# Decoder layer on one core: inputs laid out ahead of the launch, the squares of x summed from a feature-major x, the decay's clip on ScalarE

## The chip, the cores and the metric

The kernel runs on one core of a Trainium2 chip. A core has four compute engines that run their own instruction lists side by side: TensorE (PE, matrix products), VectorE (DVE), ScalarE (ACT) and GpSimd (POOL); SyncE (SP) and ACT issue transfers (DMA) from main memory into SBUF, the on-chip memory of 128 partitions. Products land in PSUM. The engines wait for one another by semaphores. The metric is the device time of one execution in microseconds (us).

## The reference

One layer of a decoder with three kinds of heads, on x of 256 tokens by 2048 features, all in float32:

```python
h = rms_norm(x, norm_w)                       # x * rsqrt(mean(x*x) + 1e-6) * w
proj = jnp.einsum('btd,de->bte', h, w_in)     # all heads' q, k, v and gates
qkv = jax.nn.silu(causal_depthwise_conv(gqkv, conv_w))
o_ret  = retention(rq, rk, rv)                # 4 heads
o_gdn  = gated_delta_rule(gq, gk, gv, g, beta)# 6 heads, chunks of 64
o_moba = moba_attention(mq, mk, mv)           # 6 heads
y = concat([rms_norm(o_ret) * silu(rg), rms_norm(o_gdn) * silu(gz), o_moba * silu(mz)])
return x + jnp.einsum('bte,ed->btd', y, w_out)
```

In the gated delta rule `decay = exp(g_cum[i] - g_cum[j])` for i >= j, and a unit lower-triangular system is solved per chunk. The norm's weights multiply features, its rsqrt multiplies tokens, so the kernel projects x * w first and scales the result by the rsqrt (`rb`) afterwards.

## The kernel before

**Precision.** Each weight tile (128 partitions x 1024) is split into a high part (`w_hi`, a rounded copy, on ACT: `high_part`, L489) and a low part (`w_lo` = raw - high, on DVE: `low_part`, L369); x is split in the same way (`hT[:, k, 0]` and `hT[:, k, 1]`). A product is high x both halves of x plus low x the high half of x.

**Streaming.** There are 160 weight tiles, 8 per group, 20 groups (16 for the heads, 4 for the output). PE runs 64 "units" per group, 8 per tile: a unit is a 512-column and a 256-column matmul in the first groups (L1532 and L1533, or L1528 and L1529 for a bank's last). The other products (gates, chunks, attention) are put between units. Every engine's order is written by hand in terms of PE's unit number: `advance(u)` issues on ACT, DVE and POOL whatever belongs before unit u. In DVE's list the low part of tile n stands at unit 8 (n - 3) + 4, in ACT's the high part at 8 (n - 3); SP loads a tile as soon as one of the 8 buffers of `w_raw` is free. Each engine works its list in sequence and stops at a wait.

**The first group** (units 0 to 63) is written apart, since x has to be prepared beside it. Token-major x is loaded into `big`, in five pieces between the tiles (`load_piece`). PE transposes it in blocks of 128 (`x_block`, L1581) into PSUM, one set of four ahead of every tile; ACT makes the high half from PSUM (`x_high`, L576), DVE the low half from PSUM and the high half (L1016); POOL adds the two back into `whole` (L864, 16 instructions of 256 columns), which the 32 narrow gate products read (`ab_products`, L1670). The sums of squares are taken from token-major x by ACT (L557, tokens 0 to 127) and DVE (L1002, tokens 128 to 255), four pieces each; DVE makes the mean (L1031), POOL the power -1/2 (L851), PE spreads it over partitions (L1659), DVE copies it to `rb` (L1033). Parameters arrive as rows (`prow`) and are turned by PE (L1629, L1675). At the end DVE adds the halves of the first products and scales them (L1040, L1042), and later ones are added and scaled on POOL (L888, L892).

**Later.** `decay_clip` (DVE, L1167) forms min(g_cum difference, 0) for four 128 x 128 blocks of a pair of heads, ACT takes the exponent (L642). `inverse_of_pairs` (DVE, L1202 and L1205) prepares the solve of a pair of heads; the solve starts at unit 290. POOL's 512-wide subtraction L868 is part of the heads' outputs at 195 us and later.

## Time and profile before

| | us |
|---|---|
| median of 3 executions (lowest, highest) | 511.75 (511.47, 512.03) |
| the profiled execution | 511.29 |
| its span, first to last instruction | 509.5 |
| PE busy | 504.4 (99%) |
| DVE busy | 342.9 (67%) |
| ACT busy | 275.5 (54%) |
| POOL busy | 162.3 (32%) |

The profiled execution lasts 1.8 us longer than its span, for what lies before the first and behind the last instruction. The granted clock of TensorE was 0.999 of full speed in the mean. A row of the timeline gives the start, the busy time of the instructions that it groups (x2, x8: so many alike in a row), engine, line, what it writes and reads with partitions x columns, and in brackets the idle time before it with what ended it. The busy spans of neighbours overlap a little: a successor may start before the row of the one ahead of it ends.

### The profile page before, as it was taken

To read this page: it belongs to the slowest core of one execution; us is meant where nothing else is said; L and a number is where in the kernel's file an instruction comes from. 1 tells how busy PE (TensorE), PEld (TensorE's weight loads), DVE (VectorE), ACT (ScalarE), POOL (GpSimd) and SP (SyncE) were. 2 spreads that over 40 slices of the span, in tenths; PEclk is the share of its full clock that TensorE was granted. 3 is DMA by queue.
4 is the path that set the end of the run, shared out by engine and by line. 5 is a ranking of instruction groups with operands and counts; after the bars stand their busy time and mean duration, and the time that the engine had idled before them with its cause. 6 is when DMAs were issued, how large, how long until landed. Compare 5 with 4: busy or idle time off the path is not lost.

```text
span 509.5 us, 8939 instructions
## 1 busy us (share of the span) xinstructions
PE 504.4 (99%) x3442; PEld 424.6 (83%) x3442; DVE 342.9 (67%) x529; ACT 275.5 (54%) x452; POOL 162.3 (32%) x220
## 2 busy tenths in 40 slices
PE   8999999999999999999999999999999999999997
PEld 7888888888888888888888888888888888888885
DVE  5989999989776876565467455755567566646451
ACT  5776565754357676564537354564556456343340
POOL 5763343416121312135054105506050614230000
PEclk9999999999999999999999999999999999999999
DMA  8997656665744465563975676777775557767711
GB/s 283 344 313 207 166 133 165 185 173 142 200 124 130 126 165 144 146 183 69 303 185 156 160 221 169 187 207 195 186 193 169 166 172 231 219 186 225 256 43 41
DMA packets 154989, 92.62 MB, mean 182 GB/s; under 512 B 15971, under 2 KB 143938, under 8 KB 154946
## 3 DMA queue, kind: packets, MB, share of 16 engines
q1 hardware_dynamic: 151456, 89.86, 63.3%
q10 hardware_dynamic: 3490, 2.18, 1.5%
q8 instruction: 27, 0.44, 0.3%
q14 instruction: 16, 0.13, 0.1%
HBM read 89.00 MB, written 2.10 MB: 179 GB/s over the span
## 4 chain that ended last, share of the span: by engine, by line
PE 99%; POOL 0%; DVE 0%; DVEq 0%; issue 0%; POOLq 0%
PE pj L1554 20%; PE pj L1557 20%; PE pj L1556 20%; PE pj L1532 14%; PE pj L1533 7%; PE pj L1610 3%; PE pj L1619 1%; PE mx L1714 1%; PE pj L1529 1%; PE mx L1581 1%; PE mx L1749 1%; PE mx L1767 1%; PE pj L1627 1%; PE mx L1825 1%; PE mx L1887 1%; PE pj L1528 1%
## 5 line engine op out<-in xcount | busy, mean ns | idle before, releaser
L369 DVE TENSOR_TENSOR w_lo<-w_raw,w_hi 128x1024 fp32r<-128x1024 f32 x160 | 200.0, 1258 | 78.0 <-ACT w_hi L489 77.3
L489 ACT ACTIVATE w_hi<-w_raw 128x1024 fp32r<-128x1024 f32 x158 | 166.1, 1057 | 120.5 <-PE pj L1557 103.7
L1554 PE MATMUL pj<-w_hi,hT 128*128 128x512 f32 x320 | 126.4, 395 | 0.0
L1556 PE MATMUL pj<-w_hi,hT 128*128 128x512 f32 x320 | 126.1, 394 | 0.0
L1557 PE MATMUL pj<-w_lo,hT 128*128 128x512 f32 x320 | 124.7, 390 | 0.0
L1532 PE MATMUL pj<-hT,w_hi 128*128 128x512 f32 x300 | 109.3, 404 | 0.0
L1533 PE MATMUL pj<-hT,w_lo 128*128 128x256 f32 x300 | 83.9, 280 | 0.0
L1557 PEld LDWEIGHTS pj<-w_lo,hT 128*128 128x128 f32 x320 | 60.1, 188 | 12.2
L1554 PEld LDWEIGHTS pj<-w_hi,hT 128*128 128x128 f32 x320 | 60.1, 188 | 12.1
L1556 PEld LDWEIGHTS pj<-w_hi,hT 128*128 128x128 f32 x320 | 60.2, 188 | 11.5
L1532 PEld LDWEIGHTS pj<-hT,w_hi 128*128 128x128 f32 x300 | 56.3, 188 | 14.1 <-DVE w_lo L369 1.6
L917 POOL COPY mT<-mT 32x128 f32<-32x128 f32 x80 | 40.4, 506 | 60.1 <-issue 45.7
L1533 PEld LDWEIGHTS pj<-hT,w_lo 128*128 128x128 f32 x300 | 56.6, 189 | 0.5
L851 POOL TENSOR_TENSOR sm<-sm,cst 128x4 f32<-128x4 f32 (+2 forms) x12 | 15.8, 1313 | 111.7 <-DVE sm L1392 39.3
L1554 PE MATMUL pj<-w_hi,yT 128*128 128x512 f32 x128 | 50.3, 393 | 0.0
L1557 PE MATMUL pj<-w_lo,yT 128*128 128x512 f32 x128 | 49.8, 389 | 0.0
L1556 PE MATMUL pj<-w_hi,yT 128*128 128x512 f32 x128 | 49.8, 389 | 0.0
L888 POOL TENSOR_TENSOR ev<-ev 128x256 f32<-128x256 f32 x22 | 23.8, 1083 | 76.0 <-ACT ev L504 76.0
L917 POOL COPY kq<-mT 32x128 f32<-32x128 f32 x56 | 32.0, 571 | 11.2 <-DVE mT L1355 8.0
L1060 DVE SCALAR_TENSOR_TENSOR big<-raw,pcol,big 128x256 f32<-128x256 f32 x54 | 33.0, 613 | 1.4
L1557 PEld LDWEIGHTS pj<-w_lo,yT 128*128 128x128 f32 x128 | 24.0, 188 | 5.1
L1556 PEld LDWEIGHTS pj<-w_hi,yT 128*128 128x128 f32 x128 | 24.0, 188 | 4.9
(238 smaller groups left out, 537.6 us busy)
## 6 DMA issues: line engine op xcount, KB each, us to landing
w_raw<-in_w_in_dram SPq DMA_DIRECT2D x256, 256.0 KB, 3.3
w_raw<-in_w_out_dram SPq DMA_DIRECT2D x64, 256.0 KB, 4.0
...
```

Source lines behind the costliest of these rows:

```text
L369: eng.tensor_tensor(w_lo[:, n % NSPLIT, :], w_raw[:, n % NRAW, :], w_hi[:, n % NSPLIT, :].bitcast(F32), ALU.subtract).then_inc(S("lo"), 1)
L489: act.activation(w_hi[:, n % NSPLIT, :], w_raw[:, n % NRAW, :], ACT.Copy).then_inc(S("hi_done"), 1)
L851: return pool.tensor_tensor(sm[:, dst:dst + n], sm[:, src:src + n], cst[:, K_POW:K_POW + n], ALU.pow)
L888: pool.tensor_tensor(ev[:, n % 2, 0:T], ev[:, n % 2, 0:T], ev[:, n % 2, T:2 * T], ALU.add).then_inc(S("halves"), 1)
L917: ins = pool.tensor_copy(dst[i:i + QUART, :, a:a + QUART], src[a:a + QUART, :, i:i + QUART])
L1060: ins = dve.scalar_tensor_tensor(dst, raw_of(j, h, i, slice(k, k + T)), tap, dst, ALU.mult, ALU.add)
L1532: pe.matmul(pj[s][:, :], high, hT[:, kc].rearrange("p a t -> p (a t)"), start=first, stop=False)
L1533: ins = pe.matmul(pj[s][:, 0:T], low, hT[:, kc, 0, :], start=False, stop=False)
L1554: ins = pe.matmul(bank[:, :], src[:, kc, 0, tok], hi[:, k, :], start=first, stop=False)
L1556: pe.matmul(bank[:, :], src[:, kc, 1, tok], hi[:, k, :], start=False, stop=False)
L1557: ins = pe.matmul(bank[:, :], src[:, kc, 0, tok], lo[:, k, :], start=False, stop=last)
L1610: pe.matmul(pj[s][:, cols], block_of(hi, 0, s, k), hT[:, TK * t + k].rearrange("p a t -> p (a t)")[:, cols], start=t == 0 and a == 0, stop ...
```

## The change

The host now lays the inputs out before the launch:

- x also goes in feature-major (`turned_x`, 128 x 4096), so that `load_piece` brings it straight into `whole`, in seven pieces; the first two are issued on ACT's queue behind the parameters. The 32 transposes of x, the first four of which stood ahead of the first product, the four `keep_busy` transposes and POOL's 16 additions L864 go. `x_high` (ACT) and `x_low` (DVE) read `whole` in SBUF in place of PSUM.
- weights come tile by tile: one transfer of 512 KB with rows of 4 KB in place of two of 256 KB; the first three tiles in two halves, whose high and low parts and products are taken by halves too.
- parameters come as columns of one array (128 x 107): no `prow`, no turning.
- the gates' weights come unpadded, and POOL multiplies them by the norm's weights into `wab` (L872), so that `ab_products` can read x itself.
- the squares of x are taken by ACT, 128 x 512 at a time, eight times (L574, into `big`). POOL adds the squares 1 to 5 onto 0 (L868), DVE adds 6 and 7 and POOL's sum (`total_squares`), PE sums over the partitions with two one-column matmuls (L1653), and the mean, power and spreading follow, the spreading in the midst of the gate products.
- the clip of the decay is a Relu on ACT with the sign turned (L642), which makes the negation of g_cum (L1114) needless; `inverse_of_pairs` of the first two pairs of heads is on POOL (units 166 and 228).

DVE's list in the first group, from tile 5's square sum on, before (L1016 is the split of x, L369 the low part of a tile, L1002 a sum of squares):

```order
L1002 SCALAR_TENSOR_TENSOR sq,sm<-big 128x512
L1016 SCALAR_TENSOR_TENSOR hT<-mx,pcol,hT 128x256 x2
L369 TENSOR_TENSOR w_lo<-w_raw,w_hi 128x1024
L1029 TENSOR_REDUCE sm<-sm 128x2
L1031 TENSOR_SCALAR sm<-sm 128x2
L1016 SCALAR_TENSOR_TENSOR hT<-mx,pcol,hT 128x256 x2
L369 TENSOR_TENSOR w_lo<-w_raw,w_hi 128x1024
L1033 COPY rb<-mx 128x256
L369 TENSOR_TENSOR w_lo<-w_raw,w_hi 128x1024
L1036 COPY pcol<-mx 128x79
```

and now, from tile 6 on (L1035 is the split, L414 the low part, L1041 to L1046 the sum of squares, L1070 the mean):

```order
L1035 SCALAR_TENSOR_TENSOR hT<-home,pcol,hT 128x256 x2
L414 TENSOR_TENSOR w_lo<-w_raw,w_hi 128x1024
L1035 SCALAR_TENSOR_TENSOR hT<-home,pcol,hT 128x256 x2
L414 TENSOR_TENSOR w_lo<-w_raw,w_hi 128x1024
L1041 TENSOR_TENSOR big<-big 128x512
L1044 TENSOR_TENSOR big<-big 128x512
L1046 TENSOR_TENSOR big<-big 128x256
L414 TENSOR_TENSOR w_lo<-w_raw,w_hi 128x1024
L1070 TENSOR_SCALAR sm<-mx 128x2
L1073 COPY rb<-mx 128x256
L1077 TENSOR_TENSOR ev<-ev 128x256
```

The squares' sums have left the places between the tiles, and the sum, now of three instructions, stands together behind the last split; the low part of tile 8, behind the copy to `rb` before, stands ahead of the mean. The split reads `home` (SBUF) in place of `mx` (PSUM).

POOL's list up to the first of its additions for the second group, before:

```order
L857 MEMSET home 128x12x32
L864 ISA
L864 TENSOR_TENSOR home<-hT 128x256 x14
L851 TENSOR_TENSOR sm<-sm,cst 128x2
L864 TENSOR_TENSOR home<-hT 128x256 x2
L888 TENSOR_TENSOR ev<-ev 128x256
```

and now (L868 is an addition of squares, L872 the scaling of the gates' weights, L856 the power):

```order
L868 ISA
L868 TENSOR_TENSOR big<-big 128x512 x2
L872 TENSOR_TENSOR wab<-sq,pcol 128x16x12
L868 TENSOR_TENSOR big<-big 128x512 x3
L856 TENSOR_TENSOR sm<-sm,cst 128x2
L901 TENSOR_TENSOR ev<-ev 128x256
```

Sixteen additions of 256 columns have become five of 512 and one scaling, all ahead of the power.

PE's list at the start of the program, before (L1610 high products, L1619 low products, L1581 transposes of x, L1588 filling ones):

```order
L1627 MATMUL pj<-er 128x256
L1629 MATMUL mx<-cst,prow 128x16
L1581 MATMUL mx<-cst,big 128x128 x4
L1588 MATMUL pj<-cst 128x128 x4
L1610 MATMUL pj<-hT,w_hi 128x256 x8
L1610 MATMUL pj<-hT,w_hi 128x512 x4
L1581 MATMUL mx<-cst,big 128x128 x4
L1619 MATMUL pj<-hT,w_lo 128x256 x8
```

and now (L1621 high, L1634 low products):

```order
L1642 MATMUL pj<-er 128x256
L1621 MATMUL pj<-hT,w_hi 128x256 x8
L1634 MATMUL pj<-hT,w_lo 128x256 x4
L1621 MATMUL pj<-hT,w_hi 128x512 x4
L1634 MATMUL pj<-hT,w_lo 128x256 x4
```

The transposes are gone, and in the first three tiles a half's low products follow its high ones. From unit 64 on PE's list is the same as before.

The diff, cut to its core:

```diff
-        X_PIECES = [(0, 2), (2, 4), (4, 8), (8, 12), (12, 16)]
-        X_LANDED = [16 * C] + [16] * (len(X_PIECES) - 1)
-        SQUARES_AT = {3: 1, 4: 2, 5: 3}
+        X_PIECES = [(0, 1), (1, 2), (2, 4), (4, 6), (6, 8), (8, 12), (12, 16)]
+        SQUARES_AT = {1: (0,), 2: (1,), 3: (2, 3), 4: (4,), 5: (5,), 6: (6, 7)}
+        X_PIECE = [i for i, (a, b) in enumerate(X_PIECES) for _ in range(a, b)]
 
         def load_piece(eng, i):
 
-            piece = slice(X_PIECES[i][0] * P, X_PIECES[i][1] * P)
-            if i:
-                eng.dma_start(x_sb[:, :, piece], x[0, :, piece].rearrange("(c p) n -> p c n", p=P)).then_inc(S(f"x_in{i}"), 16)
-                return
-            for c in range(C):
-                eng.dma_start(x_sb[:, c, piece], x[0, c * P:(c + 1) * P, piece]).then_inc(S(f"x_in{i}"), 16)
+            a, b = X_PIECES[i]
+            dst = whole(a) if b == a + 1 else home[:, (RET + GDN) * 2 * T + a * T:(RET + GDN) * 2 * T + b * T] if a < 12 else home[:, 0:4 * T]
+            eng.dma_start(dst, turned_x[:, a * T:b * T]).then_inc(S(f"x_in{i}"), 16)
+
+        def x_landed(eng, k):
+
+            eng.wait_ge(S(f"x_in{X_PIECE[k]}"), 16)
 
...
-                rows = slice(q * TK * P, (q + 1) * TK * P)
+                if n < HALVED:
+                    for k, done in enumerate((f"w_first{n}", f"w_in{n}")):
+                        cols = slice(k * 512, (k + 1) * 512)
+                        sp.dma_start(w_raw[:, n, cols], tiles[n, :, cols]).then_inc(S(done), 16)
+                    return
...
+                sp.dma_start(w_raw[:, n % NRAW, :], tiles[n]).then_inc(S(f"w_in{n % NRAW}"), 16)
...
+            X_AFTER = {0: 2, 1: 3, 2: 4, 3: 5, 5: 6}
...
-                if n in (0, 1, 3, 5):
-                    load_piece(sp, (n + 1) // 2 + 1)
+                if n in X_AFTER:
+                    load_piece(sp, X_AFTER[n])
+                if n == HALVED:
+                    sp.dma_start(wab_in, gate_w.rearrange("p (k c) -> p k c", k=KC)).then_inc(S("gates_in"), 16)
+                    sp.dma_start(cst[:, 0:K_FIRST], table[:, 0:K_FIRST]).then_inc(S("gates_in"), 16)
...
-            act.dma_start(cst[:, 0:K_FIRST], table[:, 0:K_FIRST]).then_inc(S("ident_in"), 16)
-            act.dma_start(prow[R_NORM:R_CONV, :], norm_w[0].rearrange("(k p) -> k p", p=P)).then_inc(S("ident_in"), 16)
+            act.dma_start(pcol[:, :], cols).then_inc(S("cols_in"), 16)
+            load_piece(act, 0)
+            load_piece(act, 1)
...
+            def square(b):
+
+                act.activation(x_squared(b), whole_pair(b), ACT.Square).then_inc(S("squared"), 1)
 
             def x_high(k):
 
-                act.activation(hT[:, k, 0, :], first_bank(k)[:, k % 2 * T:(k % 2 + 1) * T], ACT.Copy,
+                x_landed(act, k)
+                act.activation(hT[:, k, 0, :], whole(k), ACT.Copy,
                                scale=pcol[:, R_NORM + k:R_NORM + k + 1]).then_inc(S("h_hi"), 1)
...
-                    half_high_part(1, 1)
-                elif b == 2:
-                    high_part(2)
+                if b < HALVED:
+                    half_high_part(b, 1)
+                    if b + 1 < HALVED:
+                        half_high_part(b + 1, 0)
                 else:
                     advance(UPT * (b - LEAD + 1))
-                if b in SQUARES_AT:
-                    square_sum(SQUARES_AT[b])
-                if b in (2, 3, 4, 5):
-                    load_params(b - 2)
+                for i in SQUARES_AT.get(b, ()):
+                    if i > b:
+                        x_landed(act, 2 * i + 1)
+                    square(i)
             advance(64)
...
             def decay_exp(j):
+                act.wait_ge(S("gcb"), j + 1)
+                for n in range(4):
+                    h, c = n // 2, n % 2
+                    act.activation(dd[:, n, :], mx[3][:, n * P:(n + 1) * P], ACT.Relu, scale=-1.0,
+                                   bias=ab[:, A_GC, c, 2 * j + h:2 * j + h + 1]).then_inc(S("clip_done"), 1)
+                if j:
+                    act.wait_ge(S("er1"), j)
                 act.wait_ge(S("clip_done"), 4 * (j + 1))
-                act.activation(ee[:, :, :], dd[:, :, :], ACT.Exp).then_inc(S("exp_decay"), 1)
+                act.activation(ee[:, :, :], dd[:, :, :], ACT.Exp, scale=-1.0).then_inc(S("exp_decay"), 1)
...
-            for n in range(KC):
-                if n == KC - 2:
-                    pool.wait_ge(S("ident_in"), 2 * 16)
-                    pool.wait_ge(S("ss2"), 2)
-                    power(6, 10, 2).then_inc(S("rstd_done"), 1)
-                pool.wait_ge(S("h_lo"), n + 1)
-                pool.tensor_tensor(whole(n), hT[:, n, 0, :].bitcast(F32), hT[:, n, 1, :].bitcast(F32), ALU.add).then_inc(S("h_whole"), 1)
+            pool.wait_ge(S("cols_in"), 16)
+            for b in range(1, 6):
+                pool.wait_ge(S("squared"), b + 1)
+                if b > 1:
+                    pool.wait_ge(S("pool_step"), b - 1 + (b > 2))
+                pool.tensor_tensor(x_squared(0), x_squared(0), x_squared(b), ALU.add).then_inc(S("pool_step"), 1)
+                if b == 2:
+                    pool.wait_ge(S("gates_in"), 2 * 16)
+                    pool.wait_ge(S("pad_zero"), 2)
+                    pool.tensor_tensor(wab[:, :, 0:AB], wab_in, pcol[:, R_NORM:R_CONV].unsqueeze(2).broadcast_to([P, KC, AB]),
+                                       ALU.mult).then_inc(S("pool_step"), 1)
+            pool.wait_ge(S("norm_step"), 5)
+            power(6, 10, 2).then_inc(S("pool_step"), 1)
...
+            def inverse_of_pairs(j):
+
+                pool.wait_ge(S("mt"), 4 * j + 4)
+                pool.wait_ge(S("evac"), scaled_here[0])
+                pool.wait_ge(S("g_pow"), j + 1)
+                mine = slice(4 * j, 4 * j + 4)
+                for a in range(0, P, QUART):
...
+                    first = cst[a:a + QUART, K_FIRST_T:K_FIRST_T + QUART].unsqueeze(1).broadcast_to([QUART, 4, QUART])
+                    pool.tensor_tensor(gs[a:a + QUART, mine, :], mT[a:a + QUART, mine, a:a + QUART], first, ALU.mult).then_inc(S("moved"), 1)
...
+                stack = cst[:, K_STACK:K_STACK + QUART].unsqueeze(1).broadcast_to([P, 4, QUART])
+                pool.tensor_tensor(gs[:, mine, :], gs[:, mine, :], stack, ALU.add).then_inc(S("moved"), 1)
...
+            def x_low(k):
+
+                dve.wait_ge(S("h_hi"), k if k else 1)
+                dve.scalar_tensor_tensor(hT[:, k, 1, :], whole(k), pcol[:, R_NORM + k:R_NORM + k + 1],
+                                         hT[:, k, 0, :].bitcast(F32), ALU.mult, ALU.subtract).then_inc(S("h_lo"), 1)
+
+            def total_squares():
+
+                dve.wait_ge(S("squared"), KC // 2)
+                dve.tensor_tensor(x_squared(6), x_squared(6), x_squared(7), ALU.add).then_inc(S("norm_step"), 1)
+                dve.wait_ge(S("norm_step"), 2)
+                dve.wait_ge(S("pool_step"), 6)
+                dve.tensor_tensor(x_squared(6), x_squared(6), x_squared(0), ALU.add).then_inc(S("norm_step"), 1)
+                dve.wait_ge(S("norm_step"), 3)
+                dve.tensor_tensor(x_squared(7)[:, 0:T], x_squared(6)[:, 0:T], x_squared(6)[:, T:2 * T], ALU.add).then_inc(S("norm_step"), 1)
+
...
+            half_low_part(dve, 0, 0)
+            x_low(1)
+            half_low_part(dve, 0, 1)
+            for b in range(1, KC // 2):
+                if b < HALVED:
+                    for k in range(TK):
+                        x_low(2 * b + k)
+                        half_low_part(dve, b, k)
+                    continue
+                x_low(2 * b)
+                x_low(2 * b + 1)
+                advance(UPT * (b - LEAD) + LOW_AT + 1)
+                if b == KC // 2 - 1:
+                    total_squares()
+            advance(UPT * (KC // 2 - LEAD) + LOW_AT + 1)
             dve.wait_ge(S("norm_psum"), 1)
-            dve.tensor_copy(pcol[:, 0:KC], mx[3][:, 0:KC]).then_inc(S("norm_cols"), 1)
-            dve.wait_ge(S("norm_cols"), 1)
+            dve.tensor_scalar(sm[:, 10:12], mx[3][:, 0:C], 1.0 / D, EPS, ALU.mult, ALU.add).then_inc(S("norm_step"), 1)
+            advance(50)
             dve.wait_ge(S("norm_psum"), 2)
-            dve.tensor_scalar(hT[:, 0, 0, :], first_bank(0)[:, 0:T], pcol[:, R_NORM:R_NORM + 1], None, ALU.mult).then_inc(S("norm_cols"), 1)
...
-            def decay_clip(j):
-
-                dve.wait_ge(S("gcb"), j + 1)
-                for n in range(4):
-                    h, c = n // 2, n % 2
-                    dve.tensor_scalar(dd[:, n, :], mx[3][:, n * P:(n + 1) * P], ab[:, A_NGC, c, 2 * j + h:2 * j + h + 1], 0.0,
-                                      ALU.add, ALU.min).then_inc(S("clip_done"), 1)
...
-            all_x_blocks(0)
-            keep_busy(4)
             for t in range(TPH):
-                if t == 1:
-                    first_group_high(t, (0,))
-                    all_x_blocks(2)
-                    first_group_high(t, (1,))
-                else:
-                    first_group_high(t)
-                if t == 0:
-                    all_x_blocks(1)
+                if t < HALVED:
+                    for k in range(TK):
+                        first_group_high(t, (k,))
+                        first_group_low(t, (k,))
+                    continue
+                first_group_high(t, range(TK))
                 if t == TPH - 1:
-                    pe.wait_ge(S("rstd_done"), 1)
+                    pe.wait_ge(S("norm_step"), 4)
                     for c in range(C):
-                        ins = pe.transpose(mx[1][:, c * P:(c + 1) * P], sm[:, 6 + c:7 + c].broadcast_to([P, P]), ident)
-                    ins.then_inc(S("rb_psum"), 1)
-                first_group_low(t)
-                if t and t + 2 < KC // 2:
-                    all_x_blocks(t + 2)
+                        ins = pe.matmul(mx[3][:, c:c + 1], x_squared(7)[:, c * P:(c + 1) * P], er[:, 0, 0:1], start=True, stop=True)
+                    ins.then_inc(S("norm_psum"), 1)
+                first_group_low(t, range(TK))
             pos[0] = 64
 
-            def ab_products():
-
-                for k in range(KC // 4):
+            def ab_products(first, end):
+
+                for k in range(first, end):
                     for a in range(4):
                         ins = pe.matmul(mx[0][a * QUART:(a + 1) * QUART, 0:T], wab[:, 4 * k + a, :], whole(4 * k + a),
                                         start=k == 0, stop=k == KC // 4 - 1)
                 return ins
 
-            pe.wait_ge(S("param_in"), 5 * 16)
-            pe.transpose(mx[2][:, 0:R_ROWS], prow[:, :], ident[0:R_ROWS, 0:R_ROWS]).then_inc(S("norm_psum"), 1)
-            pe.wait_ge(S("wab_in"), 16)
-            pe.wait_ge(S("h_whole"), KC)
-            ab_products().then_inc(S("abt_psum"), 1)
+            pe.wait_ge(S("pool_step"), 3)
+            ab_products(0, 2)
+            pe.wait_ge(S("pool_step"), 7)
+            for c in range(C):
+                ins = pe.transpose(mx[1][:, c * P:(c + 1) * P], sm[:, 6 + c:7 + c].broadcast_to([P, P]), ident)
+            ins.then_inc(S("norm_psum"), 1)
+            ab_products(2, KC // 4).then_inc(S("abt_psum"), 1)
```

## Rows read from the trace of the kernel before

**Rows 1.** The page: busy us of each engine, its share and instructions.

```profile
PE 504.4 (99%) x3442; PEld 424.6 (83%) x3442; DVE 342.9 (67%) x529; ACT 275.5 (54%) x452; POOL 162.3 (32%) x220
```

**Rows 2.** Waits of PE in the whole span: engine, line, releaser, us, times, longest.

```profile
PE pj L1627 <- POOL er L853: 1.3, 1, 1.3
```

**Rows 3.** Windows: busy us (instructions) by engine, granted clock, DMA share, GB/s.

```profile
0.00:4.00 4.00, 2.69 (x4) 1.17 (x4) 0.00 (x0) 1.49 (x2) 1.95 (x9) 1.00 0.48 122
4.00:10.00 6.00, 6.00 (x39) 5.52 (x39) 4.75 (x9) 3.99 (x9) 2.60 (x3) 1.00 1.04 341
33.00:58.00 25.00, 25.00 (x161) 21.26 (x152) 24.27 (x44) 17.42 (x28) 10.03 (x10) 1.00 0.79 217
58.00:84.00 26.00, 25.98 (x151) 22.45 (x151) 25.38 (x61) 15.28 (x30) 10.64 (x9) 1.00 0.62 162
```

**Rows 4.** Timeline, DVE and PE at unit 128: start us, busy us, engine, line.

```profile
56.54 1.21 DVE L369 TENSOR_TENSOR w_lo<-w_raw,w_hi 128x1024 fp32r<-128x1024 f32 x1
...
57.47 0.39 PE L1529 MATMUL pj<-hT,w_hi 128*128 128x512 f32 x1
57.81 0.50 PE L1532 MATMUL pj<-hT,w_hi 128*128 128x512 f32 x1
```

**Rows 5.** Three lines up to 34 us (L1060: 34 to 84): ns min/median/max.

```profile
L864 POOL TENSOR_TENSOR home<-hT x16: 732/1208/1726, 6.3 to 30.2; 128x256 f32<-128x256 f32 x16
...
L1060 DVE SCALAR_TENSOR_TENSOR big<-raw,pcol,big x24: 473/486/966, 37.9 to 82.1; 128x256 f32<-128x256 f32 x24
...
L1016 DVE SCALAR_TENSOR_TENSOR hT<-mx,pcol,hT x16: 466/476/485, 5.7 to 28.0; 128x256 fp32r<-128x256 f32 x16
```

**Rows 6.** Timeline, POOL and DVE, 18 to 21 us.

```profile
18.36 2.42 POOL L864 TENSOR_TENSOR home<-hT 128x256 f32<-128x256 f32 x2 [1.04 <-DVE hT L1016]
...
17.81 0.87 DVE L1016 SCALAR_TENSOR_TENSOR hT<-mx,pcol,hT 128x256 fp32r<-128x256 f32 x2
18.60 1.58 DVE L369 TENSOR_TENSOR w_lo<-w_raw,w_hi 128x1024 fp32r<-128x1024 f32 x1
20.11 1.22 DVE L1002 SCALAR_TENSOR_TENSOR sq<-big 128x512 f32<-128x512 f32 x1
```

**Rows 7.** Timeline, PE, first product and one later period.

```profile
6.01 2.25 PE L1610 MATMUL pj<-hT,w_hi 128*128 128x256 f32 x12
...
16.01 0.60 PE L1581 MATMUL mx<-cst,big 128*128 128x128 f32 x4
16.36 2.09 PE L1610 MATMUL pj<-hT,w_hi 128*128 128x512 f32 x8
18.29 1.12 PE L1619 MATMUL pj<-hT,w_lo 128*128 128x256 f32 x8
19.60 0.95 PE L1610 MATMUL pj<-hT,w_hi 128*128 128x512 f32 x3
```

**Rows 8.** Timeline, SP's issue and ACT's first use of what it brings.

```profile
1.64 0.95 SPq L412 DMA_DIRECT2D w_raw<-in_w_in_dram  x2
...
5.33 0.63 ACT L495 ACTIVATE w_hi<-w_raw 128x512 fp32r<-128x512 f32 x1 [2.17 <-DMA w_raw<-in_w_in_dram]
```

**Rows 9.** Timeline, DVE and POOL, 209.5 to 214 us.

```profile
210.59 1.21 DVE L369 TENSOR_TENSOR w_lo<-w_raw,w_hi 128x1024 fp32r<-128x1024 f32 x1
...
210.79 2.15 POOL L868 TENSOR_TENSOR yT<-yf,yT 128x512 fp32r<-128x512 f32 x1 [7.39 <-ACT yT L638]
```

**Rows 10.** Timeline, POOL and DVE, end of the first group.

```profile
27.87 0.72 POOL L851 TENSOR_TENSOR sm<-sm,cst 128x2 f32<-128x2 f32 x1 [0.18 <-DVE sm L1031]
...
32.85 0.41 DVE L1040 TENSOR_TENSOR ev<-ev 128x256 f32<-128x256 f32 x1
```

**Rows 11.** Timeline, DVE, negation, clips and an inversion.

```profile
57.87 0.17 DVE L1114 TENSOR_SCALAR ab<-ab 128x12 f32<-128x12 f32 x1
...
64.14 1.12 DVE L1167 TENSOR_SCALAR dd<-mx,ab 128x128 f32<-128x128 f32 x4
...
75.16 1.22 DVE L1202 TENSOR_TENSOR home<-mT,cst 32x128 f32<-32x128 f32 x4
```

More of the change, by code:

```diff
@@ L62 @@
 LOW_AT = 4
+HALVED = 3
 LEVELS = 7
@@ L91 @@
 R_ROWS = R_K + 1
+R_COLS = R_ROWS + 2 * GDN
 U_SUM, U_CUM = 71, 118
@@ L133, in constants, with tile_at, section, weight_tiles @@
     return t.astype(np.float32)
-def layer(nc, x, norm_w, w_in, conv_w, a_log, dt_bias, ret_norm_w, gdn_norm_w, q_norm_w, k_norm_w, w_out,
-          table, out):
+def tile_at(n):
+    if n < HEADS * TPH:
+        return n // TPH, n % TPH
+    g, q = OUT_TILES[n - HEADS * TPH]
+    return HEADS + g, q
+def section(g, s):
+    return g % 3, s % 2, 2 * (g // 3) + s // 2
+def weight_tiles(w_in, w_out):
+    tiles = np.empty((TILES, P, TK * 512), np.float32)
+    for n in range(TILES):
+        group, q = tile_at(n)
+        rows = slice(q * TK * P, (q + 1) * TK * P)
+        if group >= HEADS:
+            g = group - HEADS
+            tile = w_out[0, rows, g * 512:(g + 1) * 512].reshape(TK, P, 512)
+        elif group == 0:
+            tile = w_in[0, rows, GDN_COL:GDN_COL + 2 * GDN * P].reshape(TK, P, 2, GDN * P)[:, :, :, 0:2 * P]
+        elif group < GDN:
+            p, h, i = section(group, q // 2)
+            at = GDN_COL + (i * GDN + 2 * p + h) * P
+            tile = w_in[0, q % 2 * UPT * P:(q % 2 + 1) * UPT * P, at:at + P].reshape(UPT, P, P)
+        else:
+            kind, j = PAIRS[group // 2]
+            heads, col = {"ret": (RET, RET_COL), "moba": (MOBA, MOBA_COL)}[kind]
+            h = 2 * j + group % 2
+            tile = w_in[0, rows, col:col + 4 * heads * P].reshape(TK, P, 4, heads * P)[:, :, :, h * P:(h + 1) * P]
+        tiles[n] = np.moveaxis(tile, 0, 1).reshape(P, TK * 512)
+    return tiles
+def columns(norm_w, conv_w, a_log, dt_bias, ret_norm_w, gdn_norm_w, q_norm_w, k_norm_w):
+    per_row = [a.reshape(-1, P).T for a in (norm_w, conv_w, ret_norm_w, gdn_norm_w, q_norm_w, k_norm_w)]
+    per_head = [np.broadcast_to(a.reshape(1, GDN), (P, GDN)) for a in (a_log, dt_bias)]
+    return np.ascontiguousarray(np.concatenate(per_row + per_head, axis=1))
+def layer(nc, x, turned_x, tiles, gate_w, cols, table, out):
     ctx = ExitStack()
@@ L953, in _ @@
             norms(0, 152)
+            advance(166)
+            inverse_of_pairs(0)
             norms(1, 208)
+            advance(228)
+            inverse_of_pairs(1)
             norms(2, 256)
```

229 lines of the change are left out of this document (67 added, 162 removed).

## Prediction, written before the changed kernel was run

> **What bounds the kernel now.** I read the page's busy times first: TensorE (PE) is busy 504.4 of 509.5 us [rows 1], and waits once, 1.3 us, before its first instruction [rows 2]. So only three things can change the time: the start of the first product (6.01), the pace up to about unit 128, or a wait that enters or leaves. Then the table by stage [rows 3]: VectorE (DVE) is busy 24.27 of 25 us from 33 to 58 and 25.38 of 26 from 58 to 84, as full as PE. Then the timeline where a group begins [rows 4]: the low part of unit 128's tile (L369, from 56.54) ends at 57.75, and unit 128's first matmul follows at 57.81, 0.34 behind the one before it. Eight 512-column matmuls in a row take 1.93 (16.36 to 18.29 in [rows 7]), 0.24 each, so a 0.1 of waiting is in there. Three later boundaries (units 192, 256, 290) have 0.41, 0.37 and 0.41, each right behind such a low part: some 0.5 of waiting together. PE and DVE run neck and neck up to 124 us; who is late at unit 128 sets the end.
>
> DVE in turn is held by GpSimd (POOL). The ranges [rows 5]: POOL's L864, 256 columns, takes 0.73 to 1.73; DVE's L1060 0.47 or 0.97. The timeline [rows 6] shows how: L864 (two in a row, 2.42) starts at 18.36; L369, started at 18.60, takes 1.58 where it takes 1.21 elsewhere; the second L864 ends at 20.78, 0.6 behind it; L1002, from 20.11, ends at 21.33, 0.55 behind that. They take turns, whoever asks first. Only the split of x, L1016, which reads x from PSUM and has one SBUF tensor, never varies (0.466 to 0.485). So here a DVE instruction with two SBUF tensors and a POOL tensor_tensor exclude one another for their whole length. The Trainium skill, "SBUF — State Buffer", section "SBUF: two separate sides", says the same: the shared pair is locked for a whole instruction. By this rule the change hurts, since it moves x to SBUF; without it, it would gain (rival A).
>
> **The first group, PE.** 32 transposes of x (a set of 4 from 16.01 to 16.36, 0.35), 5 for parameters and 4 that fill go; a tile's period of 3.24 (16.36 to 19.60) becomes 2.89 [rows 7]. The first product needs no identity and no transposes now. Half a tile was issued at 1.64 as third transfer of its queue, and ScalarE (ACT) had it at 5.33 [rows 8]; it is now first on its queue at 0.74, and x's block is second on ACT's: about 3.5 after issue, 4.2 to 4.3. With one split and two handoffs that is 4.9 for the first product, a gain of 1.1. The tiles then come at the transfers' pace, 341 GB/s [rows 3], which costs a microsecond of idling in tiles 0 and 1. Were PE alone to count, 4.9 + 8 x 2.89 + 1.0 idling + 1.9 for the gate products + 0.35 for the transposes = 31.3 for unit 64 against 34.02. This is the gain on offer; about 0.3 of it goes for handoffs: 2.4.
>
> **The first group, DVE.** In the timelines a successor starts 0.07 before a row's end, so an x split costs 0.40, a low part 1.14 (half 0.60), if not blocked. Up to tile 2 the transfers lead: columns, x to piece 3 and three tiles are 2.4 MB; with 0.49 MB by 4 us (122 GB/s) and 341 GB/s behind it they are in by 10 to 10.5. ACT then has half a tile, a square, two x splits and half a tile (0.4 to 0.5 each), DVE one split and a half: to 13.35. From there to the low part of tile 7 DVE has 10 splits and 5 low parts, 4.0 + 5.7 = 9.7, now all with two SBUF tensors. Against them stand POOL's five adds of squares, 512 columns each, and the scaling of the gates' columns, which begin when ACT's second square is there, 12.7. The add's price from L868, as wide [rows 9]: at 210.79 it takes 2.15 and ends at 212.94; L369, ahead of it, ends at 211.80, so 1.14 to 1.2 is its own. I take 1.2; the bounds are one L864 and two, 0.7 and 1.4. The scaling (192 columns) I put at 0.56, less than L864's 0.7. Together 6.6. Both sides always have work waiting, so the two lists add: 13.35 + 9.7 + 6.6 = 29.6.
>
> Then DVE sums squares (0.60, 0.60, 0.34, two handoffs): 31.35. Its second add waits for POOL's fifth, done by 23.8, so not at all; were it late, the low part of tile 8 would queue behind it. The low part of tile 8 stands ahead of the mean in the queue: 32.5. The mean 0.15, POOL's power with handoffs 0.85 [rows 10], and PE, in the midst of its 32 gate products, gives the transposes at 34.0; the copy to rb and the first add of halves end at 34.8. The same addition over the rows of before comes out 0.3 short of them; with it 35.1. Before, that first add (L1040) ended at 33.26 [rows 10]: DVE is 1.85 later. PE has the high products of tile 7 at 31.6, then two one-column matmuls, low products, gate products and transposes: unit 64 at 35.0 to 35.2, 1.0 to 1.2 later. But DVE's list from there to unit 128 is the same except for one negation (L1114, 0.2 [rows 11]), and it was full: unit 128 comes 1.65 later.
>
> **Behind the first group.** The four clips leave DVE (1.12 at 64.14) for ACT, 4 x 0.3 to 0.4 in a stage where ACT has 15.28 busy of 26: hidden. The inversions of two pairs (1.22 and an add each, from 75.16) go to POOL, 10.64 busy of 26; on POOL each of the five could cost from DVE's 0.3 to L864's 1.7 blocked, 1.5 to 8.5, and is wanted only at unit 290, over 40 us after the first and 20 us after the second: hidden too. DVE gains 2.6 before unit 192, so the waits at the last three boundaries go: -0.5; no more, as PE has no others there. Tiles in one transfer of 4 KB rows: the transfers' share is 0.79 and 0.62 and PE waits for none, so nothing. The Trainium skill, "DMA: Bandwidth & Descriptors", takes rows of 512 bytes and above as already at line rate, so by that page nothing at the start either.
>
> **The sum**: +1.65 - 0.5 = +1.15, 512.4 on the profiled execution's scale (511.29); the median of before lies 0.46 above it: 512.9. Bounds: adds at 0.7 give back the 2.5 and more, until PE's own limit decides, -2.4: 509.3. Adds at 1.4 cost 1.0 more, x splits at 0.48 instead of 0.40 another 1.0: 514.9.
>
> **Rivals.**
> A. *The port doesn't decide*: the adds fall where DVE waits anyway, or the new split isn't held. Then DVE ends its chain by 31.0 to 31.4 and PE's gain of 2.4 stands: 509.4. For it: POOL had 16 x 0.7 = 11.2 of such work in this stretch before, and now 6.6. Against: DVE's 16 splits were out of POOL's reach before, and DVE waits nearly nowhere from 16 to 34. Chance 0.27.
> B. *Adds at 1.4, always between two splits*: each 0.40 of DVE's waits for 1.4 of POOL's, and PE's low products slip with it; a third of a tile more of waiting per tile for tiles 3 to 7, +3: 514.8. For it: L868's 2.15. Against: a part of that is L369's. Chance 0.13.
> C. *It cancels*: the earlier start (1.1) and the waits that leave (0.5) pay for the port. This needs adds of 0.9 to 1.0. 511.75, within 0.5. Chance 0.12.
> D. *PE's start*: nothing stands between the two warm-up matmuls and the first product now, where transposes did. The granted clock reads 1.00 in all stretches of [rows 3]; were it halved for the first two tiles, they would cost 2.9 each more, of which DVE's lateness hides all but about 1: 513.9. Chance 0.03.
> The forecast has 0.45, from 511.6 to 514.2.
>
> **Chances.** 0.2%, 1.0 us, is about what a measurement of this kernel can tell from no change. Of the forecast 0.28 lies above +1.0 and 0.17 below; B and D add 0.16 to slower: 0.44. A is faster but for little: 0.27, and 0.01 of C. The rest, 0.28, is same. The range 509.3 to 514.8 leaves out the lower half of A and the upper half of B. The forecast and the rival on the other side hold most of the chance; the forecast's own range is 511.6 to 514.2.
>
> **What would show it.** Start: first product at 4.9. Port: POOL's add at 1.2 to 2.4; the new split L1035 no longer constant, 0.48 or up to 1.7; tile 7's low part ends near 29.6, L1077 near 35.1; unit 64 at 35.0 to 35.2; unit 128 at 59.4; from unit 192 on no boundary with 0.4. If L1035 stays at 0.48 and L1077 comes near 31, A is right. If PE waits for ACT's L642 or POOL's L962, the part behind the first group was wrong; if tiles land before 10 us or after 11, the transfers' step was.

## The result and the profile after

| | before | changed |
|---|---|---|
| median of 22 executions, us | 511.74 | 513.31 |
| lowest, highest | 511.38, 514.01 | 512.40, 515.76 |
| profiled execution (span) | 511.29 (509.5) | 512.74 (510.9) |

The ratio of the means is 1.0032, 95% interval 1.0026 to 1.0038: slower by 1.6 us (1.3 to 1.9). Forecast were 512.9 and "slower". Of the 1.6, PE's rows in the two profiles show 1.35; the rest is treated with the last experiments.

PE's waits, changed kernel (the answer to [rows 2]; columns: engine, output and line, releaser, us in total, times, longest):

```profile
PE pj L1642 <- POOL er L858: 1.3, 1, 1.3
PE pj L1621 <- DVE hT L1050: 1.3, 1, 1.3
PE pj L1634 <- DVE w_lo L414: 1.0, 1, 1.0
PE pj L1621 <- DVE hT L1035: 0.7, 2, 0.4
PE pj L1555 <- DVE w_lo L414: 0.4, 2, 0.3
```

Before had one wait. Four more groups stand here, all for DVE: x's first high half (L1050), the low part of tile 4, two splits of x, and the low parts at the start of units 112 and 128. The stages (the answer to [rows 3]):

```profile
4.00:10.00 6.00, 4.33 (x17) 3.67 (x17) 3.00 (x6) 2.88 (x7) 0.00 (x0) 1.00 0.99 345
10.00:20.00 10.00, 10.00 (x62) 8.59 (x60) 9.72 (x13) 10.00 (x19) 5.76 (x4) 1.00 1.04 419
20.00:34.00 14.00, 12.65 (x82) 9.97 (x80) 12.23 (x16) 9.40 (x15) 4.11 (x3) 1.00 0.89 340
58.00:84.00 26.00, 25.74 (x151) 22.36 (x150) 25.40 (x51) 18.36 (x39) 13.47 (x15) 1.00 0.54 180
```

PE has lost 1.7 us of busy time from 4 to 10 and 1.35 from 20 to 34. ACT is busy all ten microseconds from 10 to 20.

The timeline of DVE and POOL from 14 to 24 us, the answer to [rows 6]. L1035 is the split of x, L414 the low part of a tile, L868 an addition of squares, L872 the gates' scaling:

```profile
13.98 1.91 DVE L1035 SCALAR_TENSOR_TENSOR hT<-home,pcol,hT 128x256 fp32r<-128x256 f32 x2
15.81 2.33 DVE L414 TENSOR_TENSOR w_lo<-w_raw,w_hi 128x1024 fp32r<-128x1024 f32 x1
18.06 2.18 DVE L1035 SCALAR_TENSOR_TENSOR hT<-home,pcol,hT 128x256 fp32r<-128x256 f32 x2
20.16 2.31 DVE L414 TENSOR_TENSOR w_lo<-w_raw,w_hi 128x1024 fp32r<-128x1024 f32 x1
22.40 1.91 DVE L1035 SCALAR_TENSOR_TENSOR hT<-home,pcol,hT 128x256 fp32r<-128x256 f32 x2
24.23 1.21 DVE L414 TENSOR_TENSOR w_lo<-w_raw,w_hi 128x1024 fp32r<-128x1024 f32 x1
25.37 0.87 DVE L1035 SCALAR_TENSOR_TENSOR hT<-home,pcol,hT 128x256 fp32r<-128x256 f32 x2
```

```profile
13.53 1.68 POOL L868 TENSOR_TENSOR big<-big 128x512 f32<-128x512 f32 x1 [11.05 <-ACT big L574]
15.73 1.32 POOL L868 TENSOR_TENSOR big<-big 128x512 f32<-128x512 f32 x1 [0.52 <-ACT big L574]
17.02 1.49 POOL L872 TENSOR_TENSOR wab<-sq,pcol 128x192 f32<-128x192 f32 x1
18.66 4.98 POOL L868 TENSOR_TENSOR big<-big 128x512 f32<-128x512 f32 x3
```

The same instructions take 1.91 or 2.18 and 2.33 while POOL works (13.5 to 23.6) and 0.87 and 1.21 once it is done. The excess of the first five rows is 1.04 + 1.12 + 1.31 + 1.10 + 1.04 = 5.6 us, of the 6.6 that the prediction gave POOL's six instructions. The split, which never varied when it read PSUM [rows 5], now goes from 0.473 to 1.523. Below, "the port" is short for this exclusion of two instructions that both read SBUF, as in the prediction.

The end of the first group (the answer to [rows 7] and [rows 10]), PE and DVE:

```profile
5.55 2.04 PE L1621 MATMUL pj<-hT,w_hi 128*128 128x256 f32 x8 [1.31 <-DVE hT L1050]
...
22.53 1.21 PE L1634 MATMUL pj<-hT,w_lo 128*128 128x256 f32 x8 [0.98 <-DVE w_lo L414]
...
33.06 1.07 PE L1662 MATMUL mx<-home,wab 128*32 128x256 f32 x16
34.06 0.43 PE L1670 MATMUL mx<-cst,sm 128*128 128x128 f32 x2
34.43 1.07 PE L1662 MATMUL mx<-home,wab 128*32 128x256 f32 x16
35.43 0.50 PE L1555 MATMUL pj<-hT,w_hi 128*128 128x512 f32 x1
```

```profile
28.09 1.22 DVE L414 TENSOR_TENSOR w_lo<-w_raw,w_hi 128x1024 fp32r<-128x1024 f32 x1
...
34.53 0.42 DVE L1073 COPY rb<-mx 128x256 f32<-128x256 f32 x1 [2.24 <-PE mx L1670]
34.99 0.43 DVE L1077 TENSOR_TENSOR ev<-ev 128x256 f32<-128x256 f32 x1
```

Unit 64 starts at 35.43 against 34.02, DVE's first addition of halves at 34.99 against 32.85. DVE is 2.14 behind, PE 1.41. And unit 128, as in [rows 4]:

```profile
58.72 1.21 DVE L414 TENSOR_TENSOR w_lo<-w_raw,w_hi 128x1024 fp32r<-128x1024 f32 x1
```

```profile
59.33 0.39 PE L1552 MATMUL pj<-hT,w_hi 128*128 128x512 f32 x1
59.98 0.50 PE L1555 MATMUL pj<-hT,w_hi 128*128 128x512 f32 x1 [0.26 <-DVE w_lo L414]
```

The low part of unit 128's tile is 2.18 later than before, unit 128 2.17. DVE's lateness is handed on without a loss. PE takes it over in two steps: 0.45 at units 112 and 113, where it waits for that tile's low part, and 0.31 at unit 128.

```profile
53.14 0.50 PE L1555 MATMUL pj<-hT,w_hi 128*128 128x512 f32 x1 [0.19 <-DVE w_lo L414]
```

Following the last high product of every fourth of a group (L1529, now L1552) through both traces gives the lateness of PE by place:

| before, us | 39.9 | 57.5 | 63.7 | 77.6 | 91.7 | 109.1 | 117.3 | 131.0 | 171.3 |
|---|---|---|---|---|---|---|---|---|---|
| changed, later by | 1.41 | 1.86 | 2.18 | 2.20 | 1.84 | 1.67 | 1.49 | 1.40 | 1.35 |

It rises to DVE's figure by unit 128 and falls by 0.85 afterwards; 1.35 stay. Unit by unit, 0.78 of the fall lies in four places: 0.11 at unit 177, 0.28 at units 192 and 193, 0.13 at 248 and 249, 0.26 at 256 and 257. At unit 290 PE's step, 0.41 before, is still 0.38.

### The profile page after: what moved, and what is told of

It reads as the page before. It is cut to its first block, busy times and chain, and to the rows that moved or that the text cites. A ratio compares the mean times of both kernels' runs of the same rounds, so it can differ in the third digit from the quotient of the medians.

```text
span 510.9 us, 8690 instructions
## 1 busy us (share of the span) xinstructions
PE 502.5 (98%) x3408; PEld 421.4 (82%) x3408; DVE 338.8 (66%) x501; ACT 280.6 (55%) x465; POOL 159.7 (31%) x220
## 4 chain that ended last, share of the span: by engine, by line
PE 90%; DVE 7%; DMA 1%; ACT 1%; issue 0%; ACTq 0%; DVEq 0%
PE pj L1577 20%; PE pj L1580 20%; PE pj L1579 20%; PE pj L1555 11%; PE pj L1556 6%; DVE w_lo L414 3%; DVE big L1097 2%; DVE hT L1035 1%; DMA home<-in_x_turned_dram 1%; PE pj L1621 1%; PE mx L1708 1%; PE mx L1761 1%; PE mx L1743 1%; PE pj L1552 1%; PE pj L1634 1%; PE mx L1819 1%
## 5 line engine op out<-in xcount | busy, mean ns | idle before, releaser
L414 DVE TENSOR_TENSOR w_lo<-w_raw,w_hi 128x1024 fp32r<-128x1024 f32 x157 | 197.3, 1265 | 77.7 <-ACT w_hi L509 77.3
L856 POOL TENSOR_TENSOR sm<-sm,cst 128x4 f32<-128x4 f32 (+2 forms) x12 | 15.8, 1314 | 120.4 <-DVE sm L1420 39.3
```

The lines of the kernel that those rows point to most:

```text
L414: eng.tensor_tensor(w_lo[:, n % NSPLIT, :], w_raw[:, n % NRAW, :], w_hi[:, n % NSPLIT, :].bitcast(F32), ALU.subtract).then_inc(S("lo"), 1)
L856: return pool.tensor_tensor(sm[:, dst:dst + n], sm[:, src:src + n], cst[:, K_POW:K_POW + n], ALU.pow)
```

## The experiments

Each kernel was run beside the kernel before on the same chip; the ratio is that of the means, so it can differ a little from that of the medians. "h0" is DVE's first addition of halves (34.99 in the changed kernel).

| kernel | median | ratio to before (95%) | h0 | unit 64 |
|---|---|---|---|---|
| changed | 513.31 | 1.0032 (1.0026-1.0038) | 34.99 | 35.43 |
| n1, no additions on POOL | 510.97 | 0.9988 (0.9979-0.9997) | 32.37 | 32.80 |
| n2, additions on DVE | 511.46 | 0.9994 (0.9985-1.0003) | 32.29 | 32.73 |
| n3, POOL's additions doubled | 516.90 | 1.0100 (1.0086-1.0114) | 38.59 | 39.03 |
| n4, later edits undone | 514.61 | 1.0057 (1.0043-1.0071) | 35.10 | 35.54 |
| n5, x's second block early | 512.52 | 1.0018 (1.0009-1.0026) | 34.33 | 34.76 |
| n6, transposes of the rsqrt first | 512.42 | 1.0017 (1.0009-1.0026) | 34.06 | 35.36 |
| n7 = n2 + n6 | 511.07 | 0.9990 (0.9982-0.9998) | 32.00 | 33.30 |
| n8 = n7 + n5 | 510.13 | 0.9973 (0.9963-0.9983) | 31.55 | 32.85 |
| n9 = n8, tiles in two transfers | 510.10 | 0.9968 (0.9957-0.9980) | 32.12 | 33.42 |
| changed, tiles in two transfers | 513.65 | 1.0035 (1.0023-1.0047) | 34.77 | 35.20 |
| before + later edits | 510.72 | 0.9985 (0.9977-0.9994) | 33.24 | 34.42 |
| before + tiles laid out | 513.47 | 1.0051 (1.0032-1.0069) | 34.10 | 35.27 |

Before (34.02) and before with the later edits (34.42) have the same first group, and n8 and n9 differ in it only by the form of the transfers; yet unit 64 differs by 0.4 and 0.6. So much can one profile's start vary, and smaller differences are read from the medians.

### n1: POOL's additions left out

```diff
-            for b in range(1, 6):
-                pool.wait_ge(S("squared"), b + 1)
...
-                pool.tensor_tensor(x_squared(0), x_squared(0), x_squared(b), ALU.add).then_inc(S("pool_step"), 1)
```

> The changed kernel without POOL's five additions of squares (the sum of squares then holds only blocks 0, 6 and 7 of eight; nothing else is left out). Port theory: the additions hold the port that DVE's split of x and its low parts need, some 5.6 us of DVE's rows up to 24 us. Without them L1035 stays near 0.48, the low part of tile 7 ends near 26.4 instead of 29.3 (ACT's high parts then lead), the first addition of halves (L1077) starts near 32.0 instead of 34.99, unit 64 near 32.6 instead of 35.43, and the time is 510.3 (509.8 to 511.0), 3 below the changed kernel's 513.3. Rival, the start: the first group is late because x's second block lands at 7.6 us and ACT is full from 10 to 20 us, so the additions change nothing: 513.0 to 513.5.

Measured: 510.97, 2.3 below the changed kernel. The same stretch of DVE as above (L1029 is the split there):

```profile
13.99 0.87 DVE L1029 SCALAR_TENSOR_TENSOR hT<-home,pcol,hT 128x256 fp32r<-128x256 f32 x2
15.17 1.23 DVE L414 TENSOR_TENSOR w_lo<-w_raw,w_hi 128x1024 fp32r<-128x1024 f32 x1 [0.31 <-ACT w_hi L509]
16.61 0.89 DVE L1029 SCALAR_TENSOR_TENSOR hT<-home,pcol,hT 128x256 fp32r<-128x256 f32 x2 [0.21 <-ACT hT L579]
17.96 1.22 DVE L414 TENSOR_TENSOR w_lo<-w_raw,w_hi 128x1024 fp32r<-128x1024 f32 x1 [0.46 <-ACT w_hi L509]
```

Not one is over its free length; DVE now waits for ACT, as the theory had it, and the low part of tile 7 ends at 26.4. PE's high products of tiles 3 and 7, first in the changed kernel and then in n1:

```profile
16.23 2.02 PE L1621 MATMUL pj<-hT,w_hi 128*128 128x512 f32 x8
...
29.73 2.01 PE L1621 MATMUL pj<-hT,w_hi 128*128 128x512 f32 x8
```

```profile
15.92 2.02 PE L1614 MATMUL pj<-hT,w_hi 128*128 128x512 f32 x8
...
27.10 2.01 PE L1614 MATMUL pj<-hT,w_hi 128*128 128x512 f32 x8
```

From the first to the second PE takes 13.50 in the changed kernel and 11.18 in n1: 2.3 less, as much as the time falls. That is more than the whole loss of 1.6, so the port's hold is shown as its cause. The rival, the start alone, would have left 513.

### n2: the additions on DVE

```diff
+                add_squares(*{3: (1, 2), 4: (3,), 5: (4,), 6: (5,)}.get(b, ()))
```

> The five additions of squares on DVE, two behind the low part of tile 3 and one behind each of the next three, instead of on POOL. Port theory: an addition costs the port 0.6 on DVE and 1.27 on POOL, so 3 us of DVE's time replace about 5.6 us of being blocked; the low part of tile 7 ends at 27 to 27.5, L1077 starts near 32.8, time 511.0 (510.5 to 511.8), below before. Rival (DVE simply has too much to do in the first group, blocked or not): 3 us more of its own work, so no gain: 513 or above.

Measured: 511.46, with h0 at 32.29. An addition takes DVE 0.69, some 3.2 us of its list in all, and that costs it less than 5.6 of POOL's holds. With n1 it answers the rival "DVE has too much to do": it has, but only with what POOL takes.

### n3: POOL's work doubled

```diff
+                pool.tensor_tensor(x_squared(b), x_squared(b), x_squared(b), ALU.mult).then_inc(S("again"), 1)
+                pool.wait_ge(S("again"), b)
```

> Each of POOL's five additions has one more POOL instruction of the same shape ahead of it (it squares the block once more, so the sum of squares is another). Port theory: 5 x 1.27 = 6.3 us more on the port while DVE has work waiting, of which most is added to L1077's start: 40 to 41 instead of 34.99, and to the time: 518.5 (517 to 519.5). Rival (the port does not decide): POOL was busy 5.8 of 10 us from 10 to 20 and idle from 23.6 to 32.4, so the doubled work fits before the power: 513.3 to 513.8.

Measured: 516.90, 3.6 more than the changed kernel; h0 at 38.59, 3.6 later. The direction is the theory's, the size is not: 6.3 was expected, 5.2 for the time.

```profile
13.94 2.71 DVE L1037 SCALAR_TENSOR_TENSOR hT<-home,pcol,hT 128x256 fp32r<-128x256 f32 x2
16.58 2.06 DVE L414 TENSOR_TENSOR w_lo<-w_raw,w_hi 128x1024 fp32r<-128x1024 f32 x1
18.56 2.16 DVE L1037 SCALAR_TENSOR_TENSOR hT<-home,pcol,hT 128x256 fp32r<-128x256 f32 x2
```

A low part is now 2.06, not 2.33: the new POOL instruction has its three operands in one block and takes 1.04 at its shortest row, and DVE's excess in the seven rows up to 30 us is 9.6, 4.0 more than in the changed kernel. In these rows the two engines take turns, and DVE loses at most one POOL instruction for each of its own (1.84 for a pair of splits, 0.85 for a low part); adding the lists, as the prediction did, is the upper bound of that.

### n4: the later edits undone

```diff
-                    act.activation(dd[:, n, :], mx[3][:, n * P:(n + 1) * P], ACT.Relu, scale=-1.0,
...
+                    dve.tensor_scalar(dd[:, n, :], mx[3][:, n * P:(n + 1) * P], ab[:, A_GC, c, 2 * j + h:2 * j + h + 1], 0.0,
+                                      ALU.subtract, ALU.min).then_inc(S("clip_done"), 1)
```

> The changed kernel with the clip back on DVE (one instruction that subtracts and takes the minimum) and both inversions back on DVE, at their old places. Theory of the prediction: DVE loses the air that it got behind unit 128, the waits at the three later boundaries return, 0.5 to 0.8 in all: 513.9 to 514.1. Rival (hidden on either engine, since the first group's lateness sets the end): 513.3 within 0.2. Second rival (they cost more on ACT and POOL than they spare DVE): 512.9 or less.

Measured: 514.61, 1.3 above the changed kernel, where 0.5 to 0.8 were expected. PE's lateness stays at 2.4 to 2.5 from unit 128 to 123 us, where the changed kernel's has fallen to 1.48: 1.0 of the 1.3 is in these rows, the rest was not placed.

### n5 and n6: the start and the end of the first group

```diff
                     for k, done in enumerate((f"w_first{n}", f"w_in{n}")):
+                        if n == 0 and k == 1:
+                            load_piece(sp, 1)
```

> The changed kernel with x's second block issued on SP's queue between the two halves of tile 0 instead of third on ACT's queue; it landed at 7.6 us there, and ACT stood 3.1 us. Port theory: what follows from tile 3 on is DVE's list plus POOL's, which begin when tile 2's halves and ACT's second square are there; these come with the transfers and are not much earlier, so L1077 gains 0.2 to 0.6 and the time is 512.7 to 513.1. Rival, the start sets the first group: the 1.3 to 1.6 us that the block comes earlier pass through to unit 128: 511.8 to 512.0.

Measured: 512.52, 0.8 less, between the theory's 0.2 to 0.6 and the rival's 1.3 to 1.5: so the late block reaches DVE's list in part. ACT stood 3.1 us for it in the changed kernel, as the row below shows, and reads it at 4.80 in n5; DVE is through with tile 2 at 13.36 instead of 13.98.

```profile
7.63 0.51 ACT L579 ACTIVATE hT<-home,pcol 128x256 fp32r<-128x256 f32 x1 [3.12 <-DMA home<-in_x_turned_dram]
```

```diff
-            ab_products(0, 2)
             pe.wait_ge(S("pool_step"), 7)
...
-            ab_products(2, KC // 4).then_inc(S("abt_psum"), 1)
+            ab_products(0, KC // 4).then_inc(S("abt_psum"), 1)
```

> The changed kernel with PE's two transposes of the rsqrt ahead of all 32 gate products instead of behind 16 of them. In the changed kernel POOL's power is done at 33.1, the transposes start at 34.06, and DVE stands 2.2 us for them. If DVE's lateness at unit 128 sets the end (2.17 of shift against PE's 1.41 at unit 64), L1077 comes at 34.1 instead of 34.99, PE's own shift becomes the later of the two, and the time is 512.5 to 512.7. Rival, PE's late unit 64 sets the end: unit 64 stays at 35.4 and the time at 513.3.

Measured: 512.42, 0.9 less, and unit 64 where it was:

```profile
33.16 0.40 PE L1669 MATMUL mx<-cst,sm 128*128 128x128 f32 x2
33.49 1.93 PE L1662 MATMUL mx<-home,wab 128*32 128x256 f32 x32
35.36 0.50 PE L1555 MATMUL pj<-hT,w_hi 128*128 128x512 f32 x1
```

This is the test of "DVE, not PE, sets the end at unit 128": at unit 64 PE did not move by more than 0.1, DVE came 0.9 earlier, the time followed DVE. The waits at units 112 and 128 are gone, and unit 128 starts at 59.03 instead of 59.98.

### n7 and n8: a version faster than both

> Additions of squares on DVE (511.46 by themselves) and the transposes of the rsqrt ahead of the gate products. Without the port's hold the low products of tile 7 end at 30.4 and the power at about 30.6, so the transposes come at 30.7 instead of 31.36, L1077 at 31.6 instead of 32.29. Theory (DVE sets the end): 0.6 to 0.8 less: 510.7 to 510.9, faster than before. Rival (with the additions on DVE, PE's own list is the later): 511.3 to 511.5.

Measured: 511.07, 0.4 below n2 where 0.6 to 0.8 were expected. PE waits 0.42 for POOL's power there, so h0 is only 0.3 earlier and unit 64 is 0.6 later. The intervals of n2 and n7 overlap, so the step from one to the other is not shown by itself; n6 shows it on the changed kernel.

> As the one before, and x's second block on SP's queue between the halves of tile 0. With the additions off POOL's list nothing but the transfers, ACT's list and PE lead the first group, so an earlier start should now pass through further than in the kernel with POOL's additions: 0.3 to 0.8 less, 510.0 to 510.5. Rival (the transfers' total lets the tiles land no earlier, and the half tile behind x's block comes later): 510.7 to 510.9, no change.

Measured: 510.13, 0.9 below n7 and 1.6 below before (ratio 0.9973).

### The later edits and the tiles by themselves, on the kernel before

> The kernel before with the later edits alone: clip and negation off DVE (Relu on ACT), two inversions on POOL. In the changed kernel DVE's lateness of 2.17 at unit 128 shrinks to 1.35 by unit 290, and 2.4 stayed with these edits undone. Theory: before has the same 0.8 of waits behind unit 128 (boundaries and tile starts), and they go: 510.8 to 511.1. The prediction's size (0.5): 511.2. Rival (ACT and POOL pay for it, or PE has no such waits): 511.6 or more.

Measured: 510.72, by the medians 1.0 below before, a little past the theory's range; by the ratio 0.8, with an interval from 0.3 to 1.2, in which the prediction's 0.5 lies too. The profile settles where: against before PE gains 0.10 at unit 177, 0.29 at 192 and 193, 0.14 at 248 and 249, 0.26 at 256 and 257, 0.79 together, the same four places and the same sizes as in the changed kernel. In the kernel before no row shows them as a wait; each is a matmul or two that start a little later.

> The kernel before with pre-tiled weights alone: one transfer of 512 KB with rows of 4 KB per tile, but for the halves of tiles 0 and 1. Prediction's step: nothing, 511.7 within 0.2. Rival, from the traces since: PE stands 0.3 to 1.5 us for 'issue' in the midst of 96 or more 32-column matmuls near 125 to 139 us in five of the eight kernels with 4 KB rows, and in none of the profiles with the old rows; if large transfers hold up what PE waits for there, the median rises by 0.3 to 0.6 (512.0 to 512.3) and the spread grows from the 0.7 of before to 1.5 or more. Third possibility: the first group's tiles land earlier, 0.2 to 0.4 less.

Measured: 513.47, by the medians 1.8 more than before (2.6 by the ratio), with a spread from 512.4 to 516.4. None of the three had this. Its profile has PE 1.25 late already at unit 64. ACT's row of the same stretch, this kernel (ACTq is ACT's issue of a transfer):

```profile
13.93 4.86 ACTq L576 DMA_DIRECT2D prow<-in_conv_w_dram  x1
...
18.83 0.47 ACT L586 ACTIVATE hT<-mx,pcol 128x256 fp32r<-128x256 f32 x1 [2.63 <-issue]
```

and the kernel before:

```profile
13.52 2.71 ACTq L566 DMA_DIRECT2D prow<-in_conv_w_dram  x1
...
15.08 0.63 ACT L557 ACTIVATE kq<-big 128x512 f32<-128x512 f32 x1
...
16.65 0.47 ACT L576 ACTIVATE hT<-mx,pcol 128x256 fp32r<-128x256 f32 x1 [0.84 <-PE mx L1581]
```

ACT issues the parameters itself, and this issue takes 4.86 us instead of 2.71. What stands ahead of it in ACT's list still runs meanwhile (15.08), but what stands behind it does not start. Before, the issue was over at 16.23 and the next split of x waited for PE anyway; here ACT stands 2.63 us for it, that split comes 2.2 later, and PE waits 0.42 for a high part. PE's lateness goes from 0.41 at 16.77, ahead of all this, to 1.07 at 20.67 and 1.25 at unit 64. So about 0.7 of it stands behind this issue, the first 0.4 is within what two starts differ by, and what makes the median 1.8 and the spread 4 us stays open. That is read from one profile, not tested by an undo, and that the larger tiles in the queue lengthen the issue is an inference. In the first group, the changed kernel issues nothing on ACT after its first three transfers.

### Form of the transfers, and a stand that is not in the waits

> The best version so far (additions on DVE, transposes of the rsqrt first, x's second block early: 510.13) with each tile in two transfers of 256 KB with rows of 2 KB. If 4 KB rows bring the stand for 'issue' (1.3 us in that version's profile, after a shift of -2.0), it goes and the time is 509.6 to 509.8. Rival (that stand has nothing to do with the transfers' form): 510.1 within 0.3.

> The changed kernel with each tile in two transfers of 256 KB with rows of 2 KB in place of one of 512 KB with rows of 4 KB. Its profiled execution (512.74, no stand for 'issue') lies 0.6 under its median (513.31). If the rows bring the stand in the other executions, the median falls to 512.7 to 512.9. Rival (form of the transfers free): 513.1 to 513.5.

Measured: 510.10 and 513.65: rows of 2 or 4 KB, one transfer or two, are the same in either kernel. What I wanted to explain is this row, n8's profile:

```profile
127.93 0.69 PE L1769 MATMUL mx<-home 32*32 32x32 f32 x57 [1.33 <-issue]
```

PE stands within a run of 96 short matmuls with nothing to wait for. The profiles of nine of the twelve other kernels show such a stand, of 0.15 to 1.3 us, between 127 and 137 us, the one with the old tiles and the later edits (0.60) among them. In n3 and n9 no wait is listed, but runs of 96 take 1.22 to 1.32 instead of 1.02. n1, before and the changed kernel have neither, and the profiled executions of the last two lie 0.4 and 0.6 below their medians. So it is no part of the change that was tested, and single profiles may not be compared behind 125 us. Whether it comes a little oftener in the changed kernel, 0.2 us in the mean, stays open.

## Why the prediction was right

By its own steps:

- *The start.* Off: the first product came at 5.55, not 4.9, since x's first block landed near 5.0 (DVE's first row starts at 5.05, released by it) and not by 4.2, and the second only at 7.6. The gain of 1.1 was 0.46. n5 prices the second block at 0.8.
- *Up to tile 2*: 13.35 forecast, 13.98 measured, by the same cause: n5 has 13.36. The sum itself was loose: 0.49 MB by 4 us and 341 GB/s bring 2.4 MB in by 9.6, not by 10 to 10.5. The transfers did not decide here; ACT waits for none after 7.6 and is full.
- *The port.* Right in mechanism and in place: 29.6 forecast for the end of tile 7's low part, 29.2 measured; an addition, put at 1.2, took 1.3 free and up to 2.1 blocked. n1 takes it away (2.3 us), n3 doubles POOL's additions (3.6). But of the 6.6 only 5.6 was blocked time: the stage began 0.6 later than forecast and was 1.0 shorter, and that its end fits so well is luck. n3 shows that adding the lists overstates still more where POOL has more.
- *The chain behind it.* The transposes forecast at 34.0 stood at 34.06; h0's end forecast at 35.1 was 35.42. DVE's lateness was put at 1.85 and is 2.14. The way there is PE's: its rows show no wait from 24.06 to 34.06, so what the port costs it at tiles 3 to 5 arrives at the transposes, and DVE stands 2.24 for them.
- *Unit 128*: +1.65 forecast, +2.17 measured. I subtracted 0.2 for the negation, but it stands behind that low part in DVE's list (57.87, the low part at 56.54 in [rows 11] and [rows 4]) and could not help there. With 0.3 from the step before, that is the difference.
- *Behind the first group.* The mechanism was right, the size too small: -0.5 forecast, -0.85 in the profiles, -1.0 alone by the medians (b1_late, 0.3 to 1.2 by the interval) and -1.3 in n4. What fails is "no more, as PE has no others there": units 192 and 256 gave 0.54, more than their 0.30 of waiting, since the matmul behind the first one also started earlier; units 177 and 249, which were not counted, gave 0.24. And of the three boundaries the third, unit 290, kept its 0.38. The two errors nearly cancel: +1.65 - 0.5 = 1.15 forecast; 2.17 - 0.85 = 1.3 in the profiles.
- *The layout of the tiles costs nothing*: right for the changed kernel, for its transfers' form at least (a_halves), wrong by 1.8 us as a statement on that edit alone (b2_tiles). I looked only at who waits for a tile; the one profile points, in part, at the issue that ACT makes beside SP's.
- *Bounds and rivals.* The upper bound took 1.0 for ten splits at 0.48 instead of 0.40, which make 0.8. A's condition, a port that doesn't decide, is n1, but its price was too good: 509.4 forecast, 510.97 measured, since the start is later than assumed and PE gives the transposes late; with both mended n8 has 510.13. B did not happen: a pair of splits lost 1.04 to 1.31 together, not 1.4 each; losses of that kind (up to 1.84 for a pair) and size (3.6) came only with n3's doubled work. D's condition, a halved granted clock, is in no row (1.00), yet the first eight products took about twice their time, as told at the end.

In short, the port's hold (2.3 by itself), the late block (0.8) and the transposes of the rsqrt behind 16 gate products (0.9) cost 3.2 together, as n8 shows, which has all three mended. That outweighs the 1.6 that the rest of the change gains, 0.8 to 1.0 of it by the later edits.
